# Where the attention transposes stand among the projection's matmuls, and when VectorE scales the probabilities

## The reference

```python
q = rmsnorm(q.reshape(bsz, t, ATT_HEADS, ATT_HEAD_DIM), q_norm)
k = rmsnorm(k.reshape(bsz, t, ATT_HEADS, ATT_HEAD_DIM), k_norm)
...
logits = (jnp.einsum('bqhd,bqkhd->bhqk', qb, k_sel) * scale + jnp.moveaxis(bias, -1, 1))
p = jax.nn.softmax(logits, axis=-1).astype(v.dtype)
return jnp.einsum('bhqk,bqkhd->bqhd', p, v_sel)
```

## Time and profile before

| | |
|---|---|
| median of 3 runs | 2114.91 us |
| lowest and highest | 2110.85 and 2115.95 us |
| the profiled execution, own time | 2112.15 us |
| its span | 2110.1 us |
| attention on TensorE | about 220 to 351 us of the span |

### The profile page before, as it was taken

How to read it: one execution, slowest core, us unless ns; L and a number is a source line. 1 busy time by engine, 2 the same in 40 slices (tenths; PEclk the granted TensorE clock), 3 DMA queues, 4 the chain that set the end, 5 groups by cost and what they waited for, 6 DMA issues and landing times.

```text
span 2110.1 us, 34267 instructions
## 1 busy us (share of the span) xinstructions
PE 2099.2 (99%) x11280; PEld 1771.3 (84%) x11280; DVE 1572.2 (75%) x2805; ACT 1008.6 (48%) x1468; POOL 1276.1 (60%) x731
## 2 busy tenths in 40 slices
PE   9999999999999999999999999999999999999999
PEld 7777777887888888888888888888888888888888
DVE  6589565557663226888888888888888899988987
ACT  6343334434433446555545545555555544444543
POOL 5345334444454666676767767767767676666665
PEclk9999999999999999999999999999999999999999
DMA  6224123233333444354454544544544766655743
GB/s 211 84 74 126 61 70 99 96 101 104 103 99 125 145 143 141 124 176 135 157 166 134 169 158 143 173 147 144 169 150 148 251 229 212 211 186 189 237 128 132
DMA packets 150118, 308.74 MB, mean 146 GB/s; under 512 B 13272, under 2 KB 54424, under 8 KB 149880
## 3 DMA queue, kind: packets, MB, share of 16 engines
q1 hardware_dynamic: 103568, 250.39, 35.7%
q10 hardware_dynamic: 46440, 56.94, 8.6%
HBM read 261.64 MB, written 45.51 MB: 146 GB/s over the span
## 4 chain that ended last, share of the span: by engine, by line
PE 91%; DVE 6%; issue 1%; DMA 1%; ACT 1%; POOL 0%; ACTq 0%; SPq 0%; DVEq 0%
PE ps L873 39%; PE ps L872 20%; PE ps L684 10%; PE ps L686 9%; PE ps L685 9%; DVE work L1461 1%; DVE work L1460 1%; DVE work L1364 1%; DVE work L1363 1%; PE ps L780 1%; PE ps L766 1%; PE ps L752 0%; DVE work L1452 0%; DVE work L1439 0%; PE ps L821 0%
## 5 line engine op out<-in xcount | busy, mean ns | idle before, releaser
L873 PE MATMUL ps<-comb,fhi 128*128 128x512 f32 x3507 | 1230.4, 393 | 0.0
L872 PE MATMUL ps<-comb,flo 128*128 128x256 f32 x3507 | 984.5, 281 | 0.4 <-POOL flo L632 0.4
L873 PEld LDWEIGHTS ps<-comb,fhi 128*128 128x128 f32 x3507 | 656.8, 187 | 146.2
L632 POOL TENSOR_TENSOR flo<-raw,fhi 128x1024 fp32r<-128x1024 f32 (+2 forms) x252 | 485.0, 1935 | 358.1 <-ACT fhi L1211 357.9
L872 PEld LDWEIGHTS ps<-comb,flo 128*128 128x128 f32 x3507 | 662.0, 189 | 7.8 <-DVE ps L1820 2.9
L602 POOL TENSOR_TENSOR wlo<-raw,whi 128x512 fp32r<-128x512 f32 x260 | 361.1, 1403 | 395.4 <-ACT whi L991 344.8
L632 POOL TENSOR_TENSOR flo<-sum,fhi 128x1024 fp32r<-128x1024 f32 (+2 forms) x168 | 324.0, 1936 | 40.1 <-ACT fhi L1211 39.9
L1211 ACT ACTIVATE fhi<-ps 128x1024 fp32r<-128x1024 f32 (+2 forms) x168 | 141.8, 844 | 421.8 <-DVE ps L1702 225.4
L684 PE MATMUL ps<-hhi,whi 128*128 128x512 f32 x784 | 317.2, 405 | 2.0 <-DVE hlo L1611 2.0
L686 PE MATMUL ps<-hlo,whi 128*128 128x512 f32 x784 | 306.4, 391 | 0.0
L685 PE MATMUL ps<-hhi,wlo 128*128 128x512 f32 x784 | 305.8, 390 | 0.0
(11 more groups left out here) (246 smaller groups left out, 2644.2 us busy)
## 6 DMA issues: line engine op xcount, KB each, us to landing
raw<-w_gu SPq DMA_DIRECT2D x176, 512.0 KB, 3.8
raw<-w_in SPq DMA_DIRECT2D x196, 256.0 KB, 3.3
raw<-w_dn SPq DMA_DIRECT2D x96, 256.0 KB, 3.0
raw<-w_dn SPq DMA_DIRECT2D x64, 320.0 KB, 3.0
act_hi<-pair_sums ACTq DMA_DIRECT2D x20, 896.0 KB, 4.2
act_lo<-pair_sums ACTq DMA_DIRECT2D x20, 896.0 KB, 8.3
raw<-w_out SPq DMA_DIRECT2D x64, 256.0 KB, 3.2
comb<-act_hi SPq DMA_DIRECT2D x21, 512.0 KB, 3.9
```

What stands on the lines that cost most here:

```text
L632: nc.gpsimd.tensor_tensor(flo[s][:, 0:w], src[:, 0:w], fhi[s][:, 0:w].bitcast(F32), ALU.subtract).then_inc(f_lo_pool, 1)
L872: nc.tensor.matmul(dst[:, 0:HT], flo[s][:, w], both[:, HI, :], start=fresh and k == 0, stop=False, skip_group_check=True)
L873: ins = nc.tensor.matmul(dst, fhi[s][:, w], both, start=False, stop=k == n - 1, skip_group_check=True)
```

## The change

On TensorE and on ScalarE the condition `odd` of the transposes and of the copies that follow them becomes `not odd`: the transposes of pair at-1 now stand in the even slot 2 * at, ahead of the products by v of pair at-2 and of the logits of pair at. That is one slot earlier than before. On VectorE the prob of unit u-1 moves ahead of the log of unit u in the same slot. No operation is added or taken away, and no buffer or semaphore changes.

```diff
@@ TensorE, side @@
                 if ATT_AT <= a < ATT_AT + N_ATT + 3:
                     at, odd = divmod(a - ATT_AT, 2)
-                    if odd and 0 <= at - 1 < N_PAIR:
+                    if not odd and 0 <= at - 1 < N_PAIR:
                         u = 2 * (at - 1)
                         pe.wait_ge(att_p, u + 2)
@@ VectorE, side @@
                 if attending:
+                    u = a - ATT_AT - 1
+                    if 0 <= u < N_ATT:
+                        b, s = att_unit(u)[1], slice(u % 4, u % 4 + 1)
+                        ve.wait_ge(att_exp, u + 1)
+                        ch_.link(V.reciprocal(rinv[:, s], rsum[:, s]))
+                        x = logit[:, u % 4, 0:P * (b + 1)]
+                        V.tensor_scalar(x, x, rinv[:, s], None, ALU.mult).then_inc(att_p, 1)
                     u = a - ATT_AT
                     if u < N_ATT:
...
                         V.tensor_scalar(nmax[:, s], rmax[:, s], -1.0, None, ALU.mult).then_inc(att_max, 1)
-                    u = a - ATT_AT - 1
-                    if 0 <= u < N_ATT:
-                        b, s = att_unit(u)[1], slice(u % 4, u % 4 + 1)
-                        ve.wait_ge(att_exp, u + 1)
-                        ch_.link(V.reciprocal(rinv[:, s], rsum[:, s]))
-                        x = logit[:, u % 4, 0:P * (b + 1)]
-                        V.tensor_scalar(x, x, rinv[:, s], None, ALU.mult).then_inc(att_p, 1)
                 if q == 0 and attending:
                     read_out(t - 1)
```

## The result

The changed kernel takes 2133.07 us in the median of 6 runs (2131.30 to 2134.65), the kernel before beside it 2112.82 us (6 runs). The ratio is 1.0099, 95% interval 1.0088 to 1.0109: 20.3 us slower. I had predicted 2128.7 us in a range of 2118 to 2137. Of all executions behind this document one, of e6_both, took 4726.76 us; it is left out as slow.

The account below looks back on a forecast made before the run. TensorE was taken to bound the kernel. Waits of 5.5 (block 3), 1.4 (pairs 2, 10) and 8.2 us (special pairs), 15.1 together, less 0.8 and 0.5, gave +13.8 us: 2128.7 us, range 2118 to 2137.

Parts of the forecast that it names:

- my own band of +11 to +17: Whole kernel: the main forecast, slower by 11 to 17 us, given a chance of 0.45.
- the rival with all meetings: Attention stretch: VectorE meets GpSimd every time, block 1 pairs late too; +17.8 us, 2133; chance 0.14.
- the one with three falls of the clock: Pairs 6, 12, 14: TensorE's clock halves after each long wait, +2.7 us each; +22, 2137; chance 0.09.
- The bound and the window: Attention stretch: TensorE's waits add to the total; it gives VectorE 5.5 us for both units of a pair.
- The chain: VectorE's logs, exposed Exps and probs before the transposes: block 3 late by 1.06 us, block 2 by 0.20, others fit.
- my 0.15 + 0.90: Block 3 on VectorE: the wait for ScalarE's Exp, put at 0.90 us with 0.04 for the signal back.
- The meetings with GpSimd: VectorE's reductions held up by GpSimd's low part: lateness becomes 1.38 us for block 3, 0.69 for block 2.
- the three pairs that carry other VectorE work: Pairs 6, 12 and 14: read-outs and convolutions delay the prob; late by 3.6, 2.1 and 2.5 us, together 8.2.
- The merging: Transposes placed ahead of the products by v: saves 0.5 us in all, ends -1.5 and +1.5.
- The sum: Whole kernel: 15.1 us of lateness, less 0.8, less 0.5, gives +13.8 us.
- lateness removed: Attention stretch: the wait of the transposes already there before the change disappears, 0.8 us.

Follow-up runs that it names:

- e6_both: Changed kernel, but VectorE's prob first only in even slots, log first in odd, and its other work moved between prob and log of even slots: 2115.47 us, ratio 1.0021.
- e1_order_only: Changed kernel with transposes and copies back in the odd slot, so only VectorE's new order (prob ahead of log) remains: 2112.30 us, ratio 1.0000.
- e8_both_last: e6_both with the transposes also moved behind the logits, at the end of the even slot's block: 2108.86 us, ratio 0.9996.
- e5_psum: Changed kernel, but scaled and biased logits stay in PSUM and the masked reduction reads PSUM and SBUF: 2132.88 us, ratio 1.0089.
- e3_work_moved: Changed kernel with VectorE's read-outs, short convolution and convolution taps moved between prob and log of the next even slot: 2123.46 us, ratio 1.0056.
- e7_last: Changed kernel with the transposes moved behind the products by v and new logits, at the end of the even slot's block: 2115.89 us, ratio 1.0028.

## Why the prediction was right, and where its sizes were off

- **The number.** The measured 2133.07 lies in the range, but 2128.7 stood on a kernel before of 2114.91 us, and beside the changed kernel it took 2112.82. That helped by 2.1 us, which is luck. As a difference I had 13.8 us and measured 20.3: outside my own band of +11 to +17, above the rival with all meetings (+17.8) and short of the one with three falls of the clock (+22). What came is mostly a mixture of these two rivals.
- **The bound and the window.** A microsecond of TensorE's waiting was a microsecond of the total: right. The window of pair 3, from 243.67 to 0.23 behind 248.95, was 5.51 us, as forecast. e1_order_only and e8_both_last show the two halves of it, late VectorE without a reader in time, and early transposes with enough time, each at no cost.
- **The chain.** Block 3 was to be 1.38 us late and was 1.33 to 1.34, block 2 0.69 and was 0.70, blocks 1 and 0 fit. The Exp that VectorE sees took 1.04 us from the start of L1491 at 245.25 to the reciprocal at 246.29, which is my 0.15 + 0.90.
- **The meetings with GpSimd.** The reductions' part is confirmed by e5_psum. But in "the three pairs that carry other VectorE work" I took the middle between no meeting and all, 8.2 us, and all of them came: 10.76 us measured. In pair 6 they are these two, 1.27 in place of 0.42 us and 1.63 in place of 0.69:

```profile
270.81 1.27 DVE L1472 TENSOR_SCALAR resid<-resid,work 128x384 f32<-128x384 f32 x1
...
275.46 1.63 DVE L1499 TENSOR_TENSOR resid<-work 128x512 f32<-128x512 f32 x1
```

  For pair 14 even my upper end, 2.9, was short of 3.52: I counted one meeting and there were two. VectorE in pair 14 of the changed kernel:

```profile
345.00 0.68 DVE L1391 TENSOR_TENSOR work<-ps,sqsum 128x512 f32<-128x512 f32 x1
...
347.03 0.16 DVE L1470 RECIPROCAL work<-work 128x1 f32<-128x1 f32 x1
347.23 1.13 DVE L1472 TENSOR_SCALAR resid<-resid,work 128x384 f32<-128x384 f32 x1
...
350.44 0.75 DVE L1511 SCALAR_TENSOR_TENSOR work<-work,pc 128x512 f32<-128x512 f32 x1
...
351.30 1.26 DVE L1472 TENSOR_SCALAR resid<-resid,work 128x384 f32<-128x384 f32 x1
```

  Both scalings of 384 columns are stretched, to 1.13 and 1.26 us from 0.42.
- **The clock.** This is the step that failed. I made it a rival with a chance of 0.09 that excludes the forecast, priced at 2.7 us a time. It is a term of the sum: it comes on top of the waits that I had forecast myself. The changed trace gives its gross size: 20.0 us of stretch, less 17.25 - 0.91 = 16.3 of added lateness, plus the 0.3 that merging saves in this place, which leaves 4.0 us for two falls, beside the 3.9 counted above at half clock: 2.0 us a fall where I had 2.7, and two falls where the rival had three. Part of it comes back, since a slow TensorE gives VectorE a longer window: pair 7, right behind the first fall, is 1.08 late in place of 1.34. On balance the two falls cost the 3.0 to 3.2 us of the two runs with the idle matmuls, or some 3.6 with their later plain pairs counted. The Trainium skill (TensorE: Matmul & The Clock Gate, Part 1) says that an idle TensorE goes back to half its clock; the trace agrees, at 0.50 behind a wait of 4.45 us.
- **The merging.** I took 0.5 us of a range of 1.5 either way; by e6_both it saves about 0.3 where the changed kernel has the transposes. The 1.6 us of e8_both_last belong to another place in the block.
- **The sum.** Measured against forecast: lateness 17.25 against 15.1, lateness removed 0.91 against 0.8, merging 0.3 against 0.5, clock 4.0 against 0. That is 20.0 against 13.8 us. The direction, the place and the mechanism were right, the size low by a third: two thirds of the gap are the clock, one third the meetings with GpSimd in the three special pairs.

## What to carry to other kernels

When a reader is moved earlier, write out the whole chain from its producer's input to it, and set it against the other engine's time between the two, pair by pair; a dependent step (here the Exp) that other work used to hide is the first thing to look for. Other work in the same in-order queue should go where that queue idles anyway, and the reader to the end of its own block: with the Exp hidden again, they took 22.5 us off the changed kernel's stretch (e8_both_last), and so back to the time of the kernel before. Once you forecast waits of 2 us and more on TensorE, forecast the clock with them, as a term and not as a rival: here 3 to 4 us for two falls.

## What the runs showed of the hardware

- The clock fell to 0.50 behind waits of 4.45 us (pair 6, both traces of the changed kernel), but not with the length of the wait alone: behind 3.52 us (pair 14) it held in one execution of the changed kernel, and behind 3.53 us it fell in the next; in the second, pair 12's wait of 2.79 us left it at 1.00, in the first it did not; in e3_work_moved it fell behind 2.27 and 2.11 us, while in the trace of e7_last it held behind 2.24. It can fall before TensorE works again (pair 6) or after: in e3_work_moved it was still 1.00 from 284.60 to 286.00, with TensorE busy 1.40 of 1.40 us, and 0.50 from 287 to 289.
- A scaling L1472, one SBUF operand and one SBUF result, is held up by GpSimd like a reduction of two SBUF operands: 1.55 us in place of 0.49, with GpSimd's operation begun 0.01 us before it. The reduction with one operand in PSUM was not: 0.69 us beside GpSimd.
- Against transposes between projection matmuls, transposes directly behind the logits save 0.1 us a pair (1.6 us in e8_both_last), directly ahead of the products by v about 0.02 (0.3 us in e6_both).
